# Inputs of a two-layer decoder trunk laid out by features by the host, and their loads put on one queue

## The reference

```
h = h + 0.5 * rms_norm(swiglu(rms_norm(h, ffn1_pre_g), w_gu, w_down), ffn1_post_g)
u = rms_norm(h, mix_pre_g) @ w_in            # queries, keys, values of two attentions, two gates
h = h + rms_norm((sigmoid(g_sb) * y_sb + sigmoid(g_df) * y_df) @ w_out, mix_post_g)
h = h + 0.5 * rms_norm(swiglu(rms_norm(h, ffn2_pre_g), ...), ffn2_post_g)
e = (p[i] @ w_ple_proj) * sigmoid(rms_norm(h, ple_pre_g) @ w_ple_gate)
h = h + rms_norm(e, ple_post_g)
```

## Time and profile before

| what | value |
|---|---|
| time, median of 3 runs | 1174.19 us (1174.1 to 1174.52) |
| span of the profiled execution, first to last instruction | 1172.6 us |
| PE busy | 1164.0 us (99%) |
| DVE busy | 850.0 us (72%) |
| ACT busy | 721.0 us (61%) |
| POOL busy | 53.0 us (5%) |
| moved by DMA | 215.37 MB, mean 184 GB/s |
| mean granted TensorE clock | 0.998 of full |

### The profile page before, as it was taken

The page is one execution under the profiler, slowest core; times in us unless marked ns, Lnnn a source line. Parts: engine busy times, 40 slices in busy tenths (PEclk is TensorE's granted clock), DMA queues, the critical chain, the costliest instruction groups (busy, mean ns, idle before and its releaser), DMA issues.

```text
span 1172.6 us, 17196 instructions
## 1 busy us (share of the span) xinstructions
PE 1164.0 (99%) x6031; PEld 983.8 (84%) x6031; DVE 850.0 (72%) x1290; ACT 721.0 (61%) x1166; POOL 53.0 (5%) x124
## 2 busy tenths in 40 slices
PE   9999999999999999999999999999999999999997
PEld 7888888888888888888888888888888888888886
DVE  6766776977857776676787776678776677677666
ACT  7555556577755755555685655565776566565555
POOL 4000000000000000000100000010000010000002
PEclk9999999999999999999999999999999999999999
DMA  9656564654354555655556565746434446546550
GB/s 296 217 181 212 171 215 164 226 172 152 121 201 146 191 204 185 208 174 211 179 171 198 172 211 179 240 165 198 171 111 179 162 162 215 194 170 209 179 196 37
DMA packets 138655, 215.37 MB, mean 184 GB/s; under 512 B 6958, under 2 KB 97904, under 8 KB 138608
## 3 DMA queue, kind: packets, MB, share of 16 engines
q1 hardware_dynamic: 135808, 208.43, 52.6%
q10 hardware_dynamic: 2576, 6.29, 1.6%
q0 software_dynamic: 224, 0.04, 0.0%
HBM read 213.68 MB, written 1.05 MB: 183 GB/s over the span
## 4 chain that ended last, share of the span: by engine, by line
PE 99%; DMA 0%; DVE 0%; ACT 0%; issue 0%; POOL 0%; POOLq 0%; DVEq 0%; ACTq 0%
PE ps L1673 23%; PE ps L1546 19%; PE ps L1548 18%; PE ps L1547 18%; PE ps L1683 12%; PE ps L1916 3%; PE ps L1593 1%; PE ps L1925 1%; PE ps L1802 1%; PE ps L1817 1%; PE ps L1776 0%; PE ps L1788 0%; DMA raw<-in_w_ple_proj 0%; PE ps L1831 0%; PE ps L1838 0%; PE ps L1803 0%
## 5 line engine op out<-in xcount | busy, mean ns | idle before, releaser
L1106 DVE SCALAR_TENSOR_TENSOR w_lo<-raw,g_layer,w_hi 128x512 fp32r<-128x512 f32 (+1 forms) x504 | 356.3, 767 | 139.2 <-ACT w_hi L644 139.2
L644 ACT ACTIVATE w_hi<-raw,g_layer 128x512 fp32r<-128x512 f32 (+1 forms) x524 | 346.7, 732 | 113.6 <-PE ps L1683 97.0
L1673 PE MATMUL ps<-x_both,w_hi 128*128 128x512 f32 x1152 | 287.7, 392 | 0.0
L1673 PEld LDWEIGHTS ps<-x_both,w_hi 128*128 128x128 f32 x1152 | 209.3, 189 | 39.4 <-issue 0.4
L1546 PE MATMUL ps<-w_hi,x_both 128*128 128x512 f32 x576 | 231.6, 402 | 0.0
L1548 PE MATMUL ps<-w_hi,x_both 128*128 128x512 f32 x576 | 225.0, 391 | 0.0
L1547 PE MATMUL ps<-w_lo,x_both 128*128 128x512 f32 x576 | 224.4, 390 | 0.0
L1103 DVE TENSOR_TENSOR w_lo<-raw,w_hi 128x1024 fp32r<-128x1024 f32 x114 | 134.8, 1221 | 61.3 <-ACT w_hi L641 61.3
L641 ACT ACTIVATE w_hi<-raw 128x1024 fp32r<-128x1024 f32 x114 | 114.7, 1053 | 92.7 <-PE ps L1548 92.5
L1683 PEld LDWEIGHTS ps<-x_both,w_lo 128*128 128x128 f32 x1152 | 152.6, 191 | 8.4
L1683 PE MATMUL ps<-x_both,w_lo 128*128 128x256 f32 x1152 | 156.0, 283 | 0.0
(11 more groups left out here) (230 smaller groups left out, 1041.7 us busy)
## 6 DMA issues: line engine op xcount, KB each, us to landing
raw<-in_ffn_w_gu SPq DMA_DIRECT2D x170, 512.0 KB, 4.6
raw<-in_ffn_w_down SPq DMA_DIRECT2D x88, 512.0 KB, 4.0
raw<-in_w_in SPq DMA_DIRECT2D x80, 512.0 KB, 4.5
raw<-in_w_out SPq DMA_DIRECT2D x16, 512.0 KB, 4.1
raw<-in_w_ple_gate SPq DMA_DIRECT2D x16, 512.0 KB, 4.1
raw<-in_w_branch_sb SPq DMA_DIRECT2D x8, 512.0 KB, 4.1
raw<-in_w_branch_diff SPq DMA_DIRECT2D x8, 512.0 KB, 4.2
raw<-in_ffn_w_gu SPq DMA_DIRECT2D x12, 256.0 KB, 7.8
```

What stands on the lines that cost most here:

```text
L644: last = act.activation(w_hi[:, s, part], raw[:, s, part], ACT.Copy, scale=g_layer[:, g:g + 1])
L1106: last = dve.scalar_tensor_tensor(out=w_lo[:, s, part], in0=raw[:, s, part], scalar=g_layer[:, g:g + 1], in1=whi[:, part], op0=ALU.mult, o ...
L1673: mm = pe.matmul(dst, w_hi[:, s, cols], x_both[:, :, 4 * half + k, :], start=half == 0 and k == 0, stop=stop and k == 3, skip_group_check= ...
```

## The change

The host now hands over three arrays that it lays out by features: `x_cols` (feature within a block, block, token), `p_cols` likewise for both layers, and `gain_cols` (128 features by 2 layers by 33 columns). They come in this layout out of memory into SBUF: `x_raw` (the two halves of `x`, in the tiles `sbq_t` and `sbk_t` that are free then), `p_raw` (in `soft`) and `g_cols`. The turns of the first inputs, of `p` in both layers and of the gains by TensorE are gone. ACT and DVE read `x_raw` and `p_raw` in place of PSUM. `p` is now split by features (k) and not by tokens, and the order of the first eight groups follows. The natural `x`, which fills `h`, is loaded too, after unit 2. ACT issues no `x` any more. The gain `diff_subln_g` is scaled by POOL. The warm-up is 17 turns in one go.

```diff
-WARM_UP = (13, 3)
+WARM_UP = 17
+        p_raw = soft[:, :, 0:SEQ]
+        x_raw = [sbq_t, sbk_t]
+        def x_src(i, q, idx):
+
+            if (i, q) == (0, 0):
+                return x_raw[idx % 2][:, :, idx // 2 * P:(idx // 2 + 1) * P]
+            return bank(X_BANK[q][idx]).rearrange("p (k n) -> p k n", k=4)
...
+            if (i, q) == (0, 0):
+                eng.wait_ge(xt_in[idx % 2], 16)
...
-            def load_p(t):
-                sp_.dma_start(p_nat[:, t, :], a["p"][0, 0, t * P:(t + 1) * P, :]).then_inc(p_in[t], 16)
...
+            for k in range(2):
+                sp_.dma_start(p_raw[:, k, :], a["p_cols"][0, :, k, :]).then_inc(p_in[k], 16)
...
+            def load_x_cols(n):
+                sp_.dma_start(x_raw[n][:, :, :], a["x_cols"][:, 4 * n:4 * n + 4, :]).then_inc(xt_in[n], 16)
+
             load_pieces(U_PROJ, (1, 3))
-            for u in range(1, PIECED):
-                load_pieces(u)
+            load_x_cols(0)
+            load_pieces(1)
+            load_x_cols(1)
+            load_pieces(2)
+            for t in range(TT):
+                sp_.dma_start(h[:, t, :], a["x"][0, t * P:(t + 1) * P, :]).then_inc(h_loaded[t], 16)
+            load_pieces(3)
...
-            pool.dma_start(g_rows[64:66, :], a["diff_subln_g"]).then_inc(g_in, 16)
+            pool.dma_start(g_cols[:, :, :], a["gain_cols"][:, :, :]).then_inc(g_in, 16)
...
+            pool.wait_ge(g_in, 16)
+            for i in range(DEPTH):
+                last = pool.tensor_scalar(gain_col(i, G_SUB), gain_col(i, G_SUB), 1.0 - LAM_INIT[i], None, ALU.mult)
+            last.then_inc(sub_scaled, 1)
...
-            load_x(0)
-            load_x(2)
             act.preload_act_table_set("silu_and_others")
...
+            high_p(0, 0)
             high_piece(U_PROJ, 0)
-            high_p(0, 0, slice(0, P))
             high_piece(U_PROJ, 2)
-            high_p(0, 1, slice(P, SEQ))
+            high_p(0, 1)
             high_piece(U_PROJ, 1)
             high_piece(U_PROJ, 3)
-            load_x(1)
             high_inputs(0, 0, 0, (0,))
-            act.wait_ge(first_g, 1)
+            act.wait_ge(g_in, 16)
             high_piece(1, 0)
             high_piece(1, 1)
-            load_x(3)
...
-            keep_first_gain()
             low_inputs(0, 0, 0, (0,))
+            dve.wait_ge(g_in, 16)
             low_piece(1, 0)
             low_piece(1, 1)
-            keep_gains()
...
-                    start_layer(i + 1)
-                    dve.wait_ge(layer_g, i + 2)
...
-                if q == 0:
-                    pe.wait_ge(h_loaded[idx], 16)
-                if q == 0 and i and t == 1:
+                if q == 0 and t == 1:
                     pe.wait_ge(e_kept[1], i + 1)
...
-                before_last()
...
-            warm_up(WARM_UP[0])
-            turn_p(0, (0,))
-            warm_up(WARM_UP[1])
-            turn_p(0, (1,))
+            warm_up(WARM_UP).then_inc(units_used, SLOTS)
...
+    laid["x_cols"] = np.asarray(inputs["x"])[0].reshape(SEQ, KD, P).transpose(2, 1, 0)
+    laid["p_cols"] = np.asarray(inputs["p"])[:, 0].reshape(DEPTH, SEQ, 2, P).transpose(0, 3, 2, 1)
```

More of the change, by code:

```diff
@@ L216, in trunk_kernel @@
         x_split = sem("x_split")
-        h_loaded = [sem(f"h_loaded{n}") for n in range(2 * TT)]
+        h_loaded = [sem(f"h_loaded{t}") for t in range(TT)]
         h_ready = sem("h_ready")
@@ L284, in trunk_kernel @@
         post_in = [sem(f"post_in{s}") for s in range(2)]
-        p_in = [sem(f"p_in{t}") for t in range(TT)]
-        first_g_in = sem("first_g_in")
+        p_in = [sem(f"p_in{k}") for k in range(2)]
+        xt_in = [sem(f"xt_in{n}") for n in range(2)]
         g_in = sem("g_in")
@@ L957, in late_loads @@
                     if i < LAST:
-                        act.dma_start(p_nat[:, :, :], a["p"][i + 1, 0, :, :].rearrange("(t p) n -> p t n", p=P)
-                                      ).then_inc(p_in[0], 16)
+                        for k in range(2):
+                            act.dma_start(p_raw[:, k, :], a["p_cols"][i + 1, :, k, :]).then_inc(p_in[k], 16)
                 ffn(i, 1, U_FFN2, 16, lambda: high(i, U_GATE, 24, ks=2), late_loads)
                 if i < LAST:
-                    high_p(i + 1)
+                    for k in range(2):
+                        high_p(i + 1, k)
                 boundary(i, 2, 4, DOWN_PAIR,
@@ L1045, in _ @@
             last.then_inc(freq_set, 1)
[L1047 to L1071, removed]
-                dve.tensor_copy(g_layer[:, 0:32].rearrange("p (n k) -> p n k", n=4),
-                                g_cols[:, :, i * KD:(i + 1) * KD]).then_inc(layer_g, 1)
+            for n in range(DEPTH):
+                dve.memset(neg_inits[:, n:n + 1], -LAM_INIT[n])
             def low_piece(u, k):
@@ L1479, in _ @@
                 if i < LAST:
-                    low_p(i + 1)
+                    for k in range(2):
+                        low_p(i + 1, k)
                 boundary(i, 2, 4, DOWN_PAIR, lambda k: low_quarter(i, U_GATE + 1, 26, 2, k),
@@ L1645, in turn_last_ht, with pieced @@
                 mm.then_inc(ht_turned, 1)
-            def pieced(u, k, then=None):
+            def pieced(u, k):
                 def wait():
@@ L1745, in ffn @@
                         for t in range(TT):
-                            before = turned_at(0, 0, *{(0, 1): ((1,), (1,)), (1, 0): ((3,), (1,))}.get((s, t), ((), ())))
-                            if t == 0:
-                                before = {k: pieced(u0 + s, k, before.get(k)) for k in range(4)}
+                            before = {k: pieced(u0 + s, k) for k in range(4)} if t == 0 else None
                             mm = first_gate_up(s, t, before)
@@ L1995, in _ @@
             NEXT_INPUT = {0: 1, 3: 4}
-            def turn_p(i, tiles=range(TT)):
-                pe.wait_ge(p_in[tiles[0]], 16 * i + 16)
-                for k in range(2):
-                    for t in tiles:
-                        mm = pe.transpose(p_bank(i, t)[:, k, t * P:(t + 1) * P], p_nat[:, t, k * P:(k + 1) * P],
-                                          ident[:, :])
-                mm.then_inc(p_turned, 1)
             def warm_up(n):
                 for _ in range(n):
-                    pe.transpose(bank(HT_BANK)[:, 0:P], ident[:, :], ident[:, :])
@@ L2022, in first_proj @@
-            def first_proj():
-                beside = {(0, 1): lambda: (turn(0, 0, 0), turn_first_gain()), (0, 3): lambda: turn(0, 0, 2),
-                          (1, 3): turn_gains}
-                for t, k in ((0, 0), (0, 2), (1, 0), (1, 2), (0, 1), (0, 3), (1, 1), (1, 3)):
-                    if (t, k) in beside:
-                        beside[t, k]()
-                    if k == 0:
-                        pe.wait_ge(p_split, nth_p(0, t))
-                    if t == 0 and k < 3:
-                        pe.wait_ge(piece_split, (0, 2, 1).index(k) + 1)
-                    if (t, k) == (0, 3):
-                        begin(0, U_PROJ)
-                    cols, toks = piece(U_PROJ, k), slice(t * P, (t + 1) * P)
-                    mm = exact(bank(E_PAIR[t] + k // 2), p_hi[:, k % 2, toks], p_lo[:, k % 2, toks],
-                               w_hi[:, slot(U_PROJ), cols], w_lo[:, slot(U_PROJ), cols], k % 2 == 0, k % 2 == 1)
-                    if (t, k) == (0, 3):
-                        mm.then_inc(e_done, 1)
+                    mm = pe.transpose(bank(HT_BANK)[:, 0:P], ident[:, :], ident[:, :])
@@ new lines, in warm_up @@
+                return mm
+            def first_proj():
+                for k in (0, 2, 1, 3):
+                    for t in range(TT):
+                        if k < 2 and t == 0:
+                            pe.wait_ge(p_split, k + 1)
+                        if t == 0 and k < 3:
+                            pe.wait_ge(piece_split, (0, 2, 1).index(k) + 1)
+                        elif t == 0:
+                            begin(0, U_PROJ)
+                        cols, toks = piece(U_PROJ, k), slice(t * P, (t + 1) * P)
+                        mm = exact(bank(E_PAIR[t] + k // 2), p_hi[:, k % 2, toks], p_lo[:, k % 2, toks],
+                                   w_hi[:, slot(U_PROJ), cols], w_lo[:, slot(U_PROJ), cols], k % 2 == 0, k % 2 == 1)
+                        if (t, k) == (0, 3):
+                            mm.then_inc(e_done, 1)
@@ L2066, in _ @@
                 mixer(i)
-                ffn(i, 1, 3, U_FFN2, (lambda: turn_p(i + 1)) if i < LAST else (lambda: None))
+                ffn(i, 1, 3, U_FFN2)
                 def gate(u, s, t, before, i=i):
```

124 lines of the change are left out of this document (49 added, 75 removed).

## The result

| | before | changed |
|---|---|---|
| median of 19 runs | 1174.19 us (1173.76 to 1174.68) | 1176.15 us (1174.89 to 1177.47) |
| span of the profiled execution | 1172.6 us | 1173.9 us |
| time of the profiled execution | not given beside the page | 1175.65 us |

The ratio is 1.0018, 95% interval 1.0012 to 1.0024: slower by 1.96 us, where 1173.7 was forecast with a range up to 1175.5. The runs of the changed kernel also spread over 2.6 us, those of before over 0.9. The profiled execution is 0.5 under its own median, so its 1.3 us is the small end of the loss.

A forecast was written before the change was run, and what follows sets the result against it. PE, busy 99% of the span, was taken to bound the kernel. Unit 3's start (-0.1) and turns of p (-0.44) gave -0.5: span 1172.6 to 1172.1, plus 1.6 to the median, 1173.7 us, range 1172.0 to 1175.5.

The forecast's parts named there:

- What PE sheds: PE's stream: turns of x and about 0.5 us more go at the start, turns of p save 0.44 in layer 1.
- When PE can begin: Start: p needs no turning, so PE's first product comes at 5.95 us, 0.23 earlier.
- The bytes up to unit 1: Start, DMA: same bytes ahead, unit 1's first piece lands at 10.06 us as before; no wait worth naming.
- The waits in unit 2: Unit 2: PE waits 1.1 us before it (begins 19.0) and 1.1 before tile 1 (22.9); unit 3 begins 25.6.
- Is unit 3 ready: Unit 3 at 25.6 us: its pieces are split in time by 0.3; PE has 5.7 of unit 3 for unit 4.
- Priced at nothing: Gains transfer, POOL's scaling, small DVE and ACT copies, fewer transfers on ACT's queue: no cost claimed.
- The prize is had: Rival, start: unit 3 begins at 24.5 or 23.1 us, time 1172.6 or 1171.2; whole or in part, chance 0.27.
- The clock falls: Rival, unit 2: a PE wait lowers the clock, costing 2.4 us, time 1176.1; with other slower cases, chance 0.15.
- Late bytes: Rival, start: unit 3's piece lands at 21.0 us, unit 3 begins at 26.5, time 1174.6; chance 0.15.

The follow-up runs named there:

- e1: Changed kernel with two unused tiles that put every tile behind the gains back at its address before; 1175.21 us, ratio 1.0009.
- e4: Kernel before with 1.05 MB more (natural x once more, into free tiles) on SP's queue between units 2 and 3; 1175.41 us, ratio 1.0012.
- e7: Kernel before with only the tiles behind the gains 320 bytes lower, the gains' own tiles put at the end; 1174.89 us, ratio 1.0006.
- e6: e1 with the first half of x_cols issued on ACT's queue, not on SP's; 1175.27 us, ratio 1.0010.
- e2: Changed kernel with the two last quarters of x split before the copies of unit 0's product and before unit 3's pieces; 1175.73 us, ratio 1.0014.
- e3: Changed kernel with the natural x loaded behind unit 3, its squares behind unit 3's pieces on ACT; 1175.79 us, ratio 1.0013.
- e5: Changed kernel with e1's addresses, e2's order, e3's late natural x, and the first FFN's tile 1 product ahead of unit 4's first half; 1172.43 us, ratio 0.9985.
- e9: e5 with the natural x back ahead of unit 3 and its squares back in their place; 1173.74 us, ratio 1.0001.
- e8: Changed kernel with an unused 320-byte tile ahead of `gates`, so only tiles from there on regain their addresses before; 1175.37 us, ratio 1.0011.

## Why the prediction was wrong

**What PE sheds, right.** The turns of p of layer 1: 0.44 forecast, a shift of 1.30 that becomes 0.90 over that stretch.

**When PE can begin, right.** First product forecast at 5.95, found at 5.60; the gain was lost behind it.

**The bytes up to unit 1, mis-sized.** "Its first piece lands at 10.06 as before": it landed at about 10.6 in the profiled execution and later in others (11.8 in e1), and unit 1 began at 12.47, not 12.1. The bytes ahead were counted right; DMA moved them more slowly. In 4 to 6 us alone executions differ (347 in e4, 309 in e7, both with the loads of before up to there), but over the first 8 us the three profiles with the old loads have 236 to 240 GB/s and the eight with the new ones 210 to 223. So it belongs to the change and not to the execution. The second queue does not cure it (e6); whether the layout of x or of p or the order does it is open. (A slip beside it: from 12.1 PE would be done with unit 1 at 17.6, not 17.9; nothing hangs on it.)

**The waits in unit 2, right in kind.** Forecast at 19.0 and 22.9, found at 19.56 and 23.40, ended by the two quarters of x in ACT's order; e2 took both away. Unit 3's first piece landed at 20.6, not 20.1, and this 0.5 is the mis-sized term. By an estimate some 0.4 of it is the slow start: 1.76 MB moved in the first 8 us in place of 1.90 (from 220 and 238 GB/s), at 355 GB/s. DMA moved 371 GB/s from 17.2 to 19.8, where the natural x went, and not the 402 to 407 that I took, an estimated 0.2 for its 1.05 MB. From that landing to tile 1 of unit 2 the forecast 2.8 was right. The 358 GB/s of the Trainium skill, DMA: Bandwidth & Descriptors, Specifications, which I had set aside, would have given 20.4; that is nearer by luck, since the trace went over this figure, with 370 GB/s from 8 to 20.6 us.

**"Is unit 3 ready", the step that failed.** I asked only whether unit 3 was split and whether unit 4 would be ("PE has 5.7 us of unit 3 for it"), and held that the lag dissolves. PE's second part of unit 3 also waits for the product of tile 1. Its row ended 0.05 ahead of need in the kernel before, as long as PE takes to go on behind the same product when it does wait (0.06 in the changed kernel). No slack stood where I assumed 5.7 us. So ACT's delay behind unit 3's piece goes to PE undiminished: unit 3 began 0.62 late and its second part 0.97. e2, e3 and e4 each show the wait on this product (0.73, 0.77, 0.48), and e5 and e9, which move it ahead, are free of it; e9 has the start of the kernel before with all of the late bytes.

**"Priced at nothing", also failed.** The list had instructions only. The shrunk gain tiles moved those behind them by 320 bytes, which costs 0.35 us in each mixing, 0.7 in all. e7 puts it into the kernel before, e1 and e8 take it out of the changed one.

**What each step cost, on the profiled execution.** The span was forecast to fall by 0.5 and grew by 1.3. Of these 1.8, unit 3 begun late is 0.7, the wait for the product 0.35, and the addresses 0.7. The median missed by 2.45, since it stands 2.25 over the span and not 1.6. In the profile, then, the wait for the product is the smallest of the three; that it is the step to mend shows in e2, e3 and e9, since the gains of the other edits at the start stayed small until it was moved.

**The rivals.** "The prize is had" did not come by itself, and e5 had 1.6 of its 3.0. "The clock falls" did not happen in the profiled execution, with a granted clock of 1.00 through waits of 0.72 and 0.78, nor behind the 1.55 of e1 and the 1.58 of e6, and no run of the changed kernel has a mean clock under 0.998; two runs of e9 leave it open there. "Late bytes" was nearest in kind (unit 3 at 26.5 there, 26.29 found), with half of the start's loss. The range was also too narrow upward: it took the profiled execution's landings for those of every run.

## What to carry to other kernels

Where one engine is nearly always busy, look for the wait that is met by a few hundredths in the profile before: it is where a delay of another engine can enter, and here it took back what was won ahead of it. An edit that resizes a small tile moves all tiles allocated behind it; put an unused tile in its place and compare, before a difference far from the edit is explained. Loads that are early help only if the engine that reads them comes to them early: the order of that engine has to be written for the new landings, and two mendings that each show 0.2 to 0.4, because the next wait takes the rest, can show their worth only once that wait is moved too (e2 and e3 against e5 and e9).

## What the runs showed of the hardware

Moving the tiles behind the gains by 320 bytes, those from `gates` on among them, with no instruction changed, made the mixing of layer 0 145.2 us in place of 144.9 in every profile with the moved addresses (the changed kernel, e2, e3, e7), and 144.9 in each without (before, e1, e4, e5, e6, e9). In e8, where of these tiles only those ahead of `gates` are moved, it is 144.9 too. The products that grew are those of the three passes. 376 of the 422 read `x_both` and the weights, which had not moved, and have 0.27 of the growth; 46 read `os_hi` or `os_lo`, which had, and have 0.10. So reading a moved tile is not all of it; it may be the other engines' accesses to the moved ones, which was not tried.

In the first 8 us DMA's rate differed between executions with the same queues (402 and 347 GB/s in 4 to 6 us, before and e4). Over all 8 us it went with the loads: 236 to 240 GB/s in three profiles with the old ones, 210 to 223 in eight with the new. In these the landing of the first half of x varied from 9.8 to 11.2 us.
